# TensorE waits for both rows of a pair of V rows ahead of the first of the pair's four products

## The reference

```python
q = (hf @ w_q).reshape(t, PEER_HEADS, 2, PEER_HALF)        # 8 heads, 2 halves of 128
scores = jnp.einsum('thpd,pkd->thpk', q, sub_keys)
...
idx = (e1 * N_KEYS + e2).reshape(t, PEER_HEADS * PEER_TOPK)  # 128 of 16384 experts per token
gates = jax.nn.softmax(top_s, axis=-1).reshape(t, PEER_HEADS * PEER_TOPK)
...
act = jax.nn.gelu(jnp.einsum('td,tkd->tk', hb, u_tab[ib]), approximate=False)
y = jnp.einsum('tk,tkd->td', (gb * act), v_tab[ib])
```

## Time and profile before

| what | value |
|---|---|
| median of three runs | 3587.24 us |
| profiled execution, its own time | 3575.1 us |
| its span, first to last instruction | 3573.5 us |
| TensorE busy / VectorE / GpSimd / ScalarE | 73% / 58% / 57% / 9% of the span |
| mean granted TensorE clock | 0.868 |
| moved by DMA | 1159.13 MB, 324 GB/s over the span |

### The profile page before, as it was taken

How to read it: one execution, slowest core, us unless ns; L and a number is a source line. 1 busy time by engine, 2 the same in 40 slices (tenths; PEclk the granted TensorE clock), 3 DMA queues, 4 the chain that set the end, 5 groups by cost and what they waited for, 6 DMA issues and landing times.

```text
span 3573.5 us, 30245 instructions
## 1 busy us (share of the span) xinstructions
PE 2597.0 (73%) x8914; PEld 1022.7 (29%) x8914; DVE 2078.7 (58%) x4579; ACT 334.7 (9%) x705; POOL 2038.3 (57%) x2109
## 2 busy tenths in 40 slices
PE   7999956157857785778578857785778677765588
PEld 4444543143123212321232124212321232110121
DVE  3332032879478647865686567755875586646600
ACT  2221011001001100010001000100110011000000
POOL 1100000346766776677667766775677667777765
PEclk8999978568979997899799979897999789976699
DMA  3334320579999999999999999999999999999998
GB/s 101 106 112 148 132 80 0 208 241 393 352 388 375 409 366 373 375 410 366 369 374 409 368 384 358 410 367 360 377 410 375 373 372 409 362 396 410 409 399 349
DMA packets 351628, 1159.13 MB, mean 324 GB/s; under 512 B 43280, under 2 KB 72848, under 8 KB 350480
## 3 DMA queue, kind: packets, MB, share of 16 engines
q0 software_dynamic: 301024, 1094.89, 79.3%
q1 hardware_dynamic: 46256, 58.69, 4.9%
q10 hardware_dynamic: 4224, 4.35, 0.3%
HBM read 1128.37 MB, written 29.43 MB: 324 GB/s over the span
## 4 chain that ended last, share of the span: by engine, by line
DMA 32%; PE 16%; DVE 15%; issue 14%; POOL 9%; ACT 1%; SPq 0%; POOLq 0%; DVEq 0%; ACTq 0%
DMA ring<-in_peer_v_dram,picks_T 12%; DMA ring<-in_peer_v_dram,at_T 10%; DMA ring<-in_peer_u_dram,picks 9%; DVE ring L1180 9%; POOL ring L794 9%; PE y_psum L838 8%; PE tile_psum L901 1%; PE tile_psum L908 1%; PE tile_psum L974 1%; PE tile_psum L907 1%; DVE arena L1262 1%; PE tile_psum L865 1%; PE tile_psum L956 1%; ACT arena L1083 1%; DVE arena L1306 1%
## 5 line engine op out<-in xcount | busy, mean ns | idle before, releaser
L838 PE MATMUL y_psum<-ring,spread 128*32 128x512 f32 x4096 | 1365.2, 678 | 502.8 <-DMA ring<-in_peer_v_dram,at_T 401.3
L1180 DVE CUSTOM_DVE_ANT_0 ring<-ring,h_psum 128x1024 f32<-128x1024 f32 x1024 | 1224.7, 1219 | 368.1 <-DMA ring<-in_peer_u_dram,picks 321.8
L794 POOL DMA_INDIRECT ring<-in_peer_u_dram,picks x1024 | 965.7, 943 | 803.2 <-DVE picks L1419 314.1
L838 PEld LDWEIGHTS y_psum<-ring,spread 128*32 128x32 f32 x4096 | 279.3, 117 | 1494.6 <-DMA ring<-in_peer_v_dram,at_T 637.3
L794 POOL DMA_INDIRECT ring<-in_peer_v_dram,picks_T x544 | 579.1, 1064 | 196.8 <-issue 130.5
L794 POOL DMA_INDIRECT ring<-in_peer_v_dram,at_T x480 | 452.3, 942 | 202.9 <-issue 121.1
L324 PE MATMUL proj<-hn_T,w_blk 128*128 128x512 f32 x640 | 280.1, 597 | 1.3 <-DVE hn_T L453 1.3
L974 PE MATMUL tile_psum<-w_q,arena 128*128 128x512 f32 x512 | 235.2, 612 | 8.8 <-ACT arena L1119 8.8
L324 PEld LDWEIGHTS proj<-hn_T,w_blk 128*128 128x128 f32 x640 | 121.2, 192 | 146.9 <-issue 145.2
L1444 DVE SCALAR_TENSOR_TENSOR h_psum<-x,stat,h_psum 128x1024 f32<-128x1024 f32 x8 | 10.3, 1290 | 257.0 <-PE h_psum L847 257.0
L974 PEld LDWEIGHTS tile_psum<-w_q,arena 128*128 128x128 f32 x512 | 96.3, 194 | 145.3 <-issue 134.3
(11 more groups left out here) (217 smaller groups left out, 2228.9 us busy)
## 6 DMA issues: line engine op xcount, KB each, us to landing
ring<-in_peer_u_dram,picks POOLq DMA_INDIRECT x1024, 7.1
w_blk<-in_w_in_dram SPq DMA_DIRECT2D x20, 512.0 KB, 3.6
ch_scr<-post POOLq DMA_DIRECT2D x20, 512.0 KB, 2.9
tok_scr<-frames POOLq DMA_DIRECT2D x20, 512.0 KB, 3.8
ring<-in_peer_v_dram,picks_T POOLq DMA_INDIRECT x544, 7.3
w_q<-in_peer_w_q_dram SPq DMA_DIRECT2D x8, 1024.0 KB, 6.6
ring<-in_peer_v_dram,at_T POOLq DMA_INDIRECT x480, 7.6
arena<-tok_scr SPq DMA_DIRECT2D x8, 768.0 KB, 9.2
```

The source lines that it names most:

```text
L794: pool.indirect_dma_start(ring[:, j], None, tables[kind], bass.IndirectOffsetOnAxis(ap=at, axis=0)).then_inc(filled[j], 16)
L838: last = nc.tensor.matmul(y_ps[quad * STEPS:(quad + 1) * STEPS, half], lines[:, quad, at:at + STEPS], ring[:, j, half * BANK:(half + 1) * ...
L1180: nc.vector.tensor_tensor_reduce(out=ring[:, j], in0=ring[:, j], in1=h_ps[:], scale=1.0, scalar=0.0, op0=ALU.mult, op1=ALU.add, accum_out= ...
```

## The change

The waits for both rows of the pair now stand ahead of its first product. The products and their order, the conditions of the waits and the places where slots are given back are the same.

```diff
                 lines = spread[SPREADS[b][0]]
                 tokens = [("V", v + n, back) for n in range(2)]
+                for token in tokens:
+                    pe.wait_ge(filled[slot_of(token, e)], 16 * (turn_of(token, e) + ROUND // SLOTS * r))
                 for half in range(2):
                     for token in tokens:
                         j, quad = slot_of(token, e), token[1] % QUADS
-                        if half == 0:
-                            pe.wait_ge(filled[j], 16 * (turn_of(token, e) + ROUND // SLOTS * r))
                         last = nc.tensor.matmul(y_ps[quad * STEPS:(quad + 1) * STEPS, half], lines[:, quad, at:at + STEPS],
                                                 ring[:, j, half * BANK:(half + 1) * BANK],
                                                 start=False, stop=(step == STEPS - 1))
```

## The result

The changed kernel takes 3615.64 us (median of 5 runs, 3607.11 to 3622.33) against 3587.24 us (5 runs, 3586.83 to 3592.15): the ratio is 1.0076, interval 1.0059 to 1.0093. That is 28.4 us more, where 3.0 were forecast; it is slower by more than the 0.2% that the prediction counts as no change, and lies outside its range. The profiled execution took 3622.33 us, the slowest of the five, so stretches of this trace are read for where the time went, and medians for how much.

A forecast was written before the change was run, and what follows sets the result against it. The prediction took the DMA engines' gather of table rows at 410 GB/s as the bound. Only the changeovers added time, 3.0 us, with all other terms 0: 3587.2 + 3.0 = 3590.2 us, called "same", range 3584 to 3600.

The forecast's parts named there:

- joint pairs: Pairs where TensorE finds both rows already landed, some 130; the change was to leave them as they are, cost 0.
- 156 us or more: Sign expected in the changed profile: TensorE's busy time falls by this much, from some 380 waiting pairs.
- What the issuer makes of 0.86 us: Step pricing the first slot's later release place by place: V-only and mixed hidden, 322 GB/s part 0, changeovers 3.0 us.
- its first two points: V-only stretch: 2.9 us of slack covers 0.86; mixed stage at 410 GB/s: 3.2 us of queue covers it; both hidden.
- The mixed stages, "hidden" and "0": At 410 GB/s a late gather lands when it would have; in the 322 GB/s part waiting pairs are joint, cost 0.
- The changeovers, 3.0 us: Eight places where the ring passes between tiles: 0.86 us for the last tile, 0.3 for each of the other seven.
- The clock: TensorE's clock in V-only stretches stays up with 0.65 us of idle per pair, cost 0; upper bound 14 us.
- the prediction's own signs of being wrong: V-only clock row below 1, changeovers under 340 GB/s, or the second row's slot also coming back later.
- Rival 1: At the changeovers the issuer's push is paid in full and passed on: 7 to 14 us, 3594 to 3601; chance 0.13.
- Rival 2: The clock falls in the V-only stages where a stream hiccup adds idle: 14 us, 3601 or more; chance 0.10.
- Rival 3: Faster: a phase shift spares one long gather issue (up to 4.257 us) per tile, about 3570 us; chance 0.06.

The follow-up runs named there:

- late release alone: Kernel before with its waits and order, but the first row's slot given back only behind the second row's last product, by a tiny zero-weight product: 3609.28 us, 1.0073.
- the two traces of the changed kernel: Profiles of the change as first run (3615.64 us, ratio 1.0076) and of the same kernel repeated on another chip (3612.57 us, 1.0081).
- short holds: VectorE's long two-input instructions (L1403, L1407) split into four each: on the kernel before 3544.37 us, 0.9899; on the changed kernel 3564.66 us, 0.9953.
- The kernel that spares these pairs and some neighbours: The change everywhere except the last three pairs of each round in the V-only stages, which keep the waits of the kernel before: 3599.34 us, 1.0043.
- the zero-weight product: Changed kernel plus a TensorE product with zero weights at the first row's landing: 3604.49 us, 1.0058; with the long VectorE instructions split as well, 3566.36 us, 0.9950.
- row-by-row order: Kernel before with both products of a row right behind that row's wait: 3583.54 us, 0.9996; with the long VectorE instructions split as well, 3544.64 us, 0.9895.

## Why the prediction was wrong

**What it had right.** The first slot's release is 0.84 us ahead of the second's before, for the 0.86 worked out. The second row's landing plus 1.91 us ends the pair, 0.65 us of idle in each 2.56, the clock at 1.00 and DMA at 410 in the steady V-only part, joint pairs unchanged: all as worked out. TensorE's busy time fell by 193 us, for "156 us or more" (at 0.41 us each that is some 470 waiting pairs, not 380). And the release of the first slot was named as the one thing that could cost; the kernel with late release alone (1.0073) shows that it does.

**The step that failed: "What the issuer makes of 0.86 us", its first two points, "hidden".** The argument was that a gather issued 0.86 us late finds 3.2 us of queue and lands when it would have. That looks at one gather and not at the queue, which is shorter behind it. The issuer, at 1.24 us against 1.28, needs some 20 gathers to win 0.86 us back, and before it has, the next push comes. The queue shows it: 3.83 gathers for 4.32 ahead of the holds, 3.10 for 3.47 in the mixed stages. The sum priced each place as if the queue were full again at the next. It took 410 GB/s, the rate of the stretches that I had picked, for the rate of the stage, which was 365: 1.44 us a gather. So the queue did run low in every V-only stage: the DMA engines' share of busy time was 0.94 to 0.97 in the six, where full stretches have 1.02. What emptied it stood in the prediction, as a rival: the issue of up to 4.257 us was treated as luck that a shift could spare, and not as a drain of a fixed place, four of them in a row, behind which a missing queue shows. The cost of this step was 0 in the sum. In the V-only stages it measured 16.8 and 15.7 us in the two traces of the changed kernel, by the averages over kernels some 11. By medians the change costs 11.6 us more with the holds than without (31.9 - 20.3), or 8.1 by the first result (28.4); the interval of 1 to 17 us above goes with that.

**The mixed stages, "hidden" and "0".** Here the two traces of the changed kernel lose 23.2 and 15.6 us, the one with short holds 22.6, where the whole loss by medians is 20.3. The net wait rises by 20.5 us between the two kernels with short holds (160.1 to 180.6), as much as the time (20.3). I had weighed whether one late gather lands late; the row to read was the mean rate, 384 to 391 GB/s in each of the first six of these stages of the kernel before, so 1.35 us a gather, in which neither the DMA engines (share 0.99 or 1.00, for 1.02 or 1.03 in full stretches) nor the issuer is busy all the time. What the issuer stands longer would then be passed on wherever the queue ends. Which of the pushes in a mixed stage are passed on isn't settled.

**The changeovers, 3.0 us, mis-sized.** The issuer's waits there, beside the second, third and fourth of the earlier trace rows:

```profile
2449.95 0.94 POOL L794 DMA_INDIRECT ring<-in_peer_v_dram,at_T  x1 [4.29 <-PE y_psum L838]
...
2453.07 0.94 POOL L794 DMA_INDIRECT ring<-in_peer_u_dram,picks  x1 [0.94 <-issue]
...
3525.40 0.94 POOL L794 DMA_INDIRECT ring<-in_peer_v_dram,at_T  x1 [3.70 <-PE y_psum L838]
```

3.05 us became 4.29 and 3.45 became 3.70, while the wait two gathers on fell from 1.70 to 0.94: it takes up 0.76 of a push of 1.24, not nearly all of it. Over seven of the eight places, all but the first, the long wait and the one behind it sum to 30.9 us before and to 35.6 and 36.8 in the two traces of the changed kernel, so 4.7 and 5.9 us more. The kernel that spares these pairs and some neighbours won 0.0038, about 13 us, but its waits at these places still sum to 34.2, so most of that gain does not lie in them. The term was more than 3.0, and still the smaller part.

**The clock.** One of the prediction's own signs of being wrong, a clock row below 1 in the V-only stretches, did come. The clock stayed up only in the steady part of the V-only stages, where TensorE works 1.91 us and stands 0.65 and the clock is 1.00. The whole V-only stages had 0.98 to 1.00 before and 0.91 to 0.95 after, and in the 28 us around the holds, where TensorE stood up to 3.39 us ahead of a pair (2409.18), it fell from 1.00 to 0.84. It also fell in the mixed stage (0.91 to 0.87), in the sparse stretch (0.67 to 0.60) and over the run (0.868 to 0.838), so more of each ran at the 1.2 GHz level; pairs that had been spread over 2.32 us now take 1.91 and leave longer gaps. The Trainium skill's page "TensorE: Matmul & The Clock Gate", section "HAM oscillation — how this bites in real kernels", ties the low clock to DMA waits that are longer than the bursts of work between them. The sparse stretch and the steady V-only part agree with it. The clock's price is small here: the zero-weight product brings it back to 0.867 and the ratio from 1.0076 or 1.0081 to 1.0058, with intervals that overlap, and with short holds it brings nothing.

**The rivals.** Rival 1, the push paid in full and passed on, had the right mechanism, at 0.13, and the right reason ("never catches up within a stage"). Its price of 7 to 14 us was half of the truth or less, since it stood at the changeovers alone and left out the rest of both kinds of stage. Rival 2 was right that the clock would fall in the V-only stages where the stream hiccups, around the holds, but not on the price of 14 us: the two kernels with a late release and the clock back at 0.867 and 0.864 still lose 12.5 and 11.8 us there, for 16.8 and 15.7 with the clock down. Rival 3, faster, didn't come; but the holds on which it rested are where the time is to be had. **The better kernel:** the kernel before with short holds, 3544.37 us, ratio 0.9899, beats the kernel before by 1% and the changed one by 1.9%; with the row-by-row order as well it is 0.9895, no different.

## What to carry to other kernels

Where an issuer is hardly faster than what it feeds, the time that a transfer waits in the queue is a stock that later stops of the issuer live on: a delay that "lands on time anyway" is only free if the issuer refills the stock before the next stop, so list the stops and the rate of refill, and take the rate of the whole stage, not of its best stretch. Read an issuer's waits net of its usual gap. And a maximum far over the median (4.257 against 0.937 us) is worth a look at what else runs at that moment before anything is built on it.

## What the runs showed of the hardware that I had not expected

**VectorE holds GpSimd's issue.** The issue of an indirect gather, 0.94 us by itself, takes 3.09 to 4.25 us when it begins 0.05 us or more into a 3.49 us instruction of VectorE with two SBUF inputs, and 0.94 beside a 3.49 us reduction with one. Cut to a quarter of the length, the holds in the rows shown are 1.42 to 1.62 us and the kernel is 36 us faster. The Trainium skill's page "SBUF — State Buffer", section "Who interferes with whom", says that a VectorE instruction with two SBUF inputs contends with a GpSimd instruction that reads SBUF and that a reduction never does; both agree. It also reports a probe in which such a two-input instruction did not stall a DMA; for these indirect gathers the trace shows that it holds the issue, by 2.2 to 3.3 us each, and the measurement decides.

**One of the chips used took 3947 us for the kernel that takes 3580 to 3587 on the others**, 10% more. There, the change for the current tile's rows alone showed no cost (0.9996, 0.9966 to 1.0025), where it costs 1.0031 (1.0015 to 1.0047) elsewhere; the intervals overlap. Short holds were worth the same (0.989 and 0.9899). I didn't look for the reason.
